# Hybrid attention and mLSTM layer on one Trainium2 core: the stages ahead of the MLP planned in 72 half-group slots

## What is computed

```python
xn = rmsnorm(x, ln1_w); z = xn @ w_in             # 28 column tiles of 128, and 8 gate columns
# z = [qa | ka | va | qm | km | vm | om | gates], four tiles each
# group A, 8 heads x 64: causal softmax attention over blocks of 256 (prompt: all of the past),
#   samples: top-3 blocks of the 1024 cached positions (8 pages of 128) and their own token
# group B, 4 heads x 128: mLSTM
qk = einsum('td,sd->ts', q, k) * W                # W = exp(D - m), causal
num = qk @ v + decay * (q @ C); den = qk.sum(-1) + decay * (q @ n)
h = num / maximum(abs(den), exp(-m)); C_new = dec_end * C + (w_end * k).T @ v
h = h * rsqrt(mean(h * h) + eps) * mlstm_norm_w * sigmoid(om)
x = x + concat(attn, h) @ w_out                   # 8 column tiles
x = x + square(relu(rmsnorm(x, ln2_w) @ w_up)) @ w_down   # 64 groups of 1024 x 128
y = rmsnorm(x, lnf_w)                             # also out: K, V, C, n, m of prompt and samples
```

## Time and profile before

| | |
|---|---|
| median, lowest and highest of 3 runs | 781.17, 781.05, 782.01 us |
| the profiled execution: its own time, its span | 782.44 us, 780.7 us |
| TensorE (PE) busy, granted clock | 96% of the span, 0.984 |
| VectorE (DVE), ScalarE (ACT), GpSimd (POOL) busy | 51%, 31%, 26% |
| read from and written to HBM | 92.92 MB, 6.64 MB |

### The profile page before, as it was taken

One profiled execution on the slowest core, in us unless ns is written; L12 is line 12 of the kernel. 1 busy time (PEld: TensorE's weight loads), 2 busy tenths in 40 slices (PEclk: granted clock), 3 DMA queues, 4 the chain that ended last, 5 costly groups with the idle time before them and its releaser, 6 DMA issues.

```text
span 780.7 us, 14774 instructions
## 1 busy us (share of the span) xinstructions
PE 750.3 (96%) x5781; PEld 696.1 (89%) x5781; DVE 397.2 (51%) x703; ACT 243.6 (31%) x407; POOL 204.3 (26%) x146
## 2 busy tenths in 40 slices
PE   6999998999999999889999999999989999999995
PEld 5999998979988755559999999999989999999994
DVE  3278987658876777432335433343333343343433
ACT  6242222133123444333524311333113321233213
POOL 4207996655332200013423200121002210022001
PEclk9999999789999999999999999999999999999998
DMA  6618876655421376663214233223322223313102
GB/s 219 214 58 255 264 240 218 206 147 184 132 96 61 103 207 215 193 225 113 89 34 147 66 100 108 87 76 108 109 76 90 77 87 108 109 56 108 55 1 110
DMA packets 84430, 100.54 MB, mean 129 GB/s; under 512 B 5262, under 2 KB 65250, under 8 KB 84362
## 3 DMA queue, kind: packets, MB, share of 16 engines
q1 hardware_dynamic: 73430, 92.91, 37.7%
q10 hardware_dynamic: 10932, 6.67, 2.8%
HBM read 92.92 MB, written 6.64 MB: 128 GB/s over the span
## 4 chain that ended last, share of the span: by engine, by line
PE 81%; DVE 5%; issue 4%; DMA 4%; SPq 3%; POOL 2%; ACT 1%; ACTq 0%; POOLq 0%; DVEq 0%
PE acc L593 23%; PE acc L594 23%; PE acc L595 23%; DMA kv<-in_cache_v_dram 2%; SPq L518 1%; PE acc L828 1%; SPq L524 1%; PE scr L894 1%; DMA raw<-in_w_in_dram 1%; PE scr L852 1%; POOL prod L1363 1%; PE scr L754 1%; PE scr L724 1%; PE scr L769 1%; PE scr L874 1%
## 5 line engine op out<-in xcount | busy, mean ns | idle before, releaser
L593 PE MATMUL acc<-act_hi,w_hi 128*128 128x260 f32 x960 | 275.7, 287 | 5.8 <-POOL w_lo L1007 3.0
L594 PE MATMUL acc<-act_lo,w_hi 128*128 128x260 f32 x960 | 273.3, 285 | 0.0
L595 PE MATMUL acc<-act_hi,w_lo 128*128 128x260 f32 x960 | 273.1, 284 | 0.0
L593 PEld LDWEIGHTS acc<-act_hi,w_hi 128*128 128x128 f32 x960 | 183.1, 191 | 8.3 <-issue 4.3
L1007 DVE TENSOR_TENSOR w_lo<-raw,w_hi 128x1024 fp32r<-128x1024 f32 x86 | 128.2, 1491 | 111.2 <-ACT w_hi L1000 109.7
L594 PEld LDWEIGHTS acc<-act_lo,w_hi 128*128 128x128 f32 x960 | 183.2, 191 | 0.4 <-issue 0.4
L595 PEld LDWEIGHTS acc<-act_hi,w_lo 128*128 128x128 f32 x960 | 183.1, 191 | 0.0
L1000 ACT ACTIVATE w_hi<-raw 128x1024 fp32r<-128x1024 f32 x100 | 105.2, 1054 | 182.8 <-PE acc L595 156.5
L593 PE MATMUL acc<-h_hi,w_hi 128*128 128x260 f32 x512 | 144.6, 282 | 0.0
L594 PE MATMUL acc<-h_lo,w_hi 128*128 128x260 f32 x512 | 144.5, 282 | 0.0
L595 PE MATMUL acc<-h_hi,w_lo 128*128 128x260 f32 x512 | 144.4, 282 | 0.0
(11 more groups left out here) (270 smaller groups left out, 820.0 us busy)
## 6 DMA issues: line engine op xcount, KB each, us to landing
kv<-in_cache_k_dram SPq DMA_DIRECT2D x64, 256.0 KB, 3.4
kv<-in_cache_v_dram SPq DMA_DIRECT2D x64, 256.0 KB, 3.0
raw<-in_w_up_dram SPq DMA_DIRECT2D x16, 1024.0 KB, 5.4
raw<-in_w_down_dram SPq DMA_DIRECT2D x16, 1024.0 KB, 5.1
raw<-in_w_in_dram SPq DMA_DIRECT2D x14, 1024.0 KB, 6.1
x_tok<-in_x_prompt_dram SPq DMA_DIRECT2D x8, 512.0 KB, 5.4
raw<-in_w_out_dram SPq DMA_DIRECT2D x4, 1024.0 KB, 5.1
Cs<-in_state_C_dram ACTq DMA_DIRECT2D x8, 256.0 KB, 5.8
```

Of the source, the lines that this page charges most:

```text
L593: pe.matmul(out, w_hi[:, slot, k, :], hi[k][:, cols], start=(n == 0), stop=False)
L594: pe.matmul(out, w_hi[:, slot, k, :], lo[k][:, cols], start=False, stop=False)
L595: mm = pe.matmul(out, w_lo[:, slot, k, :], hi[k][:, cols], start=False, stop=(n == KT - 1))
```

## The change

`plan()` makes one list for each of 72 **slots**. Slots 0 to 55 are the halves of the groups of `w_in`, slots 56 to 71 those of `w_out`, of which the first four are (28, half 0), (29, half 0), (28, half 1), (29, half 1). The order of `w_in` is now q, k, v of the attention, then q, k, v of each mLSTM head in turn, then the out-gates.

- Two heads of a tile `t` are attended together: `att_s` alternates between them, each on its 64 rows and with a bank of its own; one instruction adds the mask, takes the maximum and writes to SBUF; `att_p` normalises in SBUF; `att_t` are PE transposes; `att_o` alternates too, 64 wide each, into the two halves of one bank. Tiles start at slots 12, 20, 28 and 36.
- The mLSTM heads run from slots 27, 33, 39 and 45, 32 score chunks are in slots 10 to 31, `pv` in two halves of four pages in slots 38 to 55, the samples' mLSTM in 46 to 57. All 8 states have a place of their own; they are loaded in slots 31 and 45.
- `acc` is used as a ring of three banks; the fourth is for `pv`.
- VectorE makes the low parts up to group 19, GpSimd from group 20 (before: from 28).
- The out-gate is one `Sigmoid` on ScalarE and one multiply. High and low part of the mix are written where they are made.
- SP's loads are sorted by slot: weights, pages of keys and of values, two pages at a time.

```diff
-IN_ORDER = [c + t for c in (QA, QM, KM, VM, KA, VA, OM) for t in range(4)]
+COL = list(range(12)) + [c + h for h in range(MH) for c in (12, 16, 20)] + list(range(24, 28))
-DVE_LO = 28
+POOL_LO = 20
+HALVES = [(g, half) for g in range(N_IN) for half in range(2)]
+HALVES += [(G_OUT, 0), (G_OUT + 1, 0), (G_OUT, 1), (G_OUT + 1, 1)]
+HALVES += [(g, half) for g in range(G_OUT + 2, G_MLP) for half in range(2)]
+def chunk_slot(n):
+    return 10 + (2 * n + 1) // 3
+def pv_slot(b):
+    return 38 + 12 * b // 5
@@ plan
-    at(1, ("gates",))
-    at(2, ("rows",))
-    at(3, ("rows_m",))
-    at(4, ("qs_tok",), ("rows_end",))
-    at(5, ("qb", 0), ("qb", 1), ("gcols",))
+    at(2, ("gates", 0))
+    at(3, ("gates", 1))
+    at(4, ("rows",))
+    at(6, ("rows_m",))
+    at(8, ("qs_tok",), ("rows_end",))
+    at(9, ("qb", 0), ("qb", 1), ("gcols",))
+    for t in range(4):
+        at(11 + 2 * t, ("tokk", t))
+        at((18, 20, 23, 30)[t], ("tokv", t))
+        s = 12 + 8 * t
+        for n in range(3):
+            at(s + n, ("att_s", t, n))
+        for e in range(2):
+            at(s + 3 + e, ("att_p", t, e))
+            at(s + 5 + e, ("att_t", t, e))
...
+    at(33, ("gate",))
+    at(34, ("mx_t",), ("own",))
...
+    at(pv_slot(7) + 3, ("pv_end",))
...
+    at(57, ("sm_end",))
+    for n in range(4 * NS):
+        at(chunk_slot(n), ("score", *divmod(n, 4)))
+    for t in range(4):
+        at(20 + 8 * t, ("att_o", t), ("mix_att", t))
@@ PE
+            def half_gemm(i, parts, k_ready=None):
+                g, half = HALVES[i]
+                pe.wait_ge(s_w_lo_ok, g + 1)
+                if i >= 3:
+                    pe.wait_ge(s_acc_evac, i - 2)
+                for k in range(KT):
+                    if k_ready is not None:
+                        k_ready(k)
+                    three(acc[:, i % 3, 0:HALF], g % WSLOTS, parts, token_half(half), k, k)
@@ PE, qs_tok (unchanged; z_ready(g) is 2 * (g + 1))
                     pe.wait_ge(s_acc_evac, z_ready(QA + 3))
@@ PE, att_s
+                    outs = [open_job(pe, "att_s", t, n, e) for e in range(2)]
+                    for i, col in STEPS[n]:
+                        w = (i + 1) * P
+                        for e in range(2):
+                            lo = 64 * e
+                            mm = pe.matmul(outs[e][:, col:col + w], zT[lo:lo + 64, QA + t, i * P:(i + 1) * P],
                                            zT[lo:lo + 64, KA + t, 0:w], start=True, stop=True)
@@ PE, att_t and att_o
-                                mm = pe.matmul(out[:, col:col + P],
-                                               pr[:, h % 2, P_COL[i] + j * P:P_COL[i] + (j + 1) * P],
-                                               p_norm[:, h % 2, i, :], start=True, stop=True)
+                                mm = pe.transpose(out[:, col:col + P],
+                                                  pr[:, e, P_COL[i] + j * P:P_COL[i] + (j + 1) * P], ident[:, :])
-                        mm = pe.matmul(out[:, j * P:SEQ], v_tok[:, j, pair], pT[:, A_COL[j]:A_COL[j] + SEQ - j * P],
-                                       start=(j == 0), stop=(j == NT - 1))
+                        for e in range(2):
+                            mm = pe.matmul(out[64 * e:64 * e + 64, j * P:SEQ], v_tok[:, t % 2, j, 64 * e:64 * e + 64],
+                                           pTs[e][:, A_COL[j]:A_COL[j] + SEQ - j * P],
+                                           start=(j == 0), stop=(j == NT - 1))
@@ ScalarE, out-gate
-                    act.activation(o, o, ACT.Exp, scale=-1.0).then_inc(s_om_exp, 1)
+                    act.activation(zT[:, OM + h, :], zT[:, OM + h, :], ACT.Sigmoid).then_inc(s_om_sig, 1)
@@ VectorE, att_s and att_p
+                            ins = dve.tensor_tensor_reduce(
+                                out=pr[:, e, P_COL[i]:P_COL[i] + w], in0=out[:, col:col + w],
+                                in1=causal[:, SEQ - w:SEQ], scale=-ASCALE, scalar=-MASKED, op0=ALU.add, op1=ALU.min,
+                                accum_out=nmax[:, e, i:i + 1])
+                    for i in range(NT):
+                        p = pr[:, e, P_COL[i]:P_COL[i] + (i + 1) * P]
+                        ins = dve.tensor_scalar(p, p, rrec[:, e, i:i + 1], None, ALU.mult)
@@ VectorE, order of a slot
+            for s in range(N_HALVES):
+                n = s // 2 + AHEAD
+                if s % 2 == 0 and n < POOL_LO:
+                    weight_lo(dve, n, n % WSLOTS, n // 2 % 2)
+                if s < 2 * N_IN:
+                    evac_copy(s)
+                else:
+                    evac_out(s)
+                for name in TASKS[s]:
+                    task(*name)
@@ PE, ahead of slot 58
+                    if HALVES[i] == (G_OUT, 1):
+                        pe.wait_ge(s_smp_mix, 3)
```

More of the change, by code:

```diff
@@ new lines, with slot_of, z_ready, ml @@
+HALVES = [(g, half) for g in range(N_IN) for half in range(2)]
+HALVES += [(G_OUT, 0), (G_OUT + 1, 0), (G_OUT, 1), (G_OUT + 1, 1)]
+HALVES += [(g, half) for g in range(G_OUT + 2, G_MLP) for half in range(2)]
+N_HALVES = len(HALVES)
+LATE_X = 2
+def slot_of(g, half):
+    return HALVES.index((g, half))
+def z_ready(g):
+    return 2 * (g + 1)
+def ml(part, h):
+    return ML + 3 * h + part
+UNIT_PARTS = [1 if COL[2 * r + 1] == COL[2 * r] + 1 else 2 for r in range(N_IN // 2)] + [1] * (N_OUT // 2)
@@ L407, in build @@
         s_sm_pow = sem("sm_pow")
-        s_sm_end = sem("sm_end")
         s_ml_tri = sem("ml_tri")
@@ L493, in build @@
         Y_FIRST = {12: (0, 1), 13: (2, 3), 14: (NT,)}
+        HI = [QA + t for t in range(4)] + [ml(KM, h) for h in range(MH)]
+        LO = [KA + t for t in range(4)] + [ml(VM, h) for h in range(MH)]
         x_parts = tiles(act_hi), tiles(act_lo)
         h_parts = tiles(h_hi), tiles(h_lo)
-        mix_parts = tiles(mix_hi), tiles(mix_lo_att) + tiles(mix_lo_ml)
+        mix_parts = [mix[:, n, :] for n in HI], [mix[:, n, :] for n in LO]
         @block.sync
@@ L605, in main @@
                     bank_free(1)
-                    for n, k in enumerate(order):
-                        k_ready(n)
-                        three(0, n, k)
-                        three(1, n, k)
+                    for k in range(KT):
+                        k_ready(k)
+                        part(0, k)
+                        part(1, k)
                     return
@@ L612, in main @@
                     bank_free(half)
-                    for n, k in enumerate(order):
-                        if half == 0 and first_half is not None:
-                            first_half(n)
-                        three(half, n, k)
+                    for k in range(KT):
+                        part(half, k)
                     if half == 0 and between is not None:
@@ L1347, in task @@
             def task(name, *a):
-                if name == "weights":
-                    n = a[0] + AHEAD
-                    weight_lo(pool, n, n % WSLOTS, n // 2 % 2)
-                elif name == "rows":
-                    full(pool, "gates", 1)
-                    pool.memset(vm_tok[:, :, :, MD:MD + 1], 1.0).then_inc(s_vm_ones, 1)
-                elif name == "score":
+                if name == "score":
                     b, c = a
```

1107 lines of the change are left out of this document (559 added, 548 removed).

## The result

The changed kernel took 778.45 us (median of 10 runs, 775.87 to 780.5), the kernel before, on the same chips, 782.1 (10 runs, 780.57 to 783.84): ratio 0.9948, 95% interval 0.9929 to 0.9967. It is faster by 0.5%. The forecast was 760, and the range ended at 778. The profiled execution took 777.48 us; its span is 775.7.

A forecast was written before the change was run, and what follows sets the result against it. PE's own work was taken as the bound: 341 us ahead of the MLP plus 8, 12, 7 and 5 make 373, with 386.6 for the MLP 759.6 of span, median 760. Range 751 to 769; 8 in 10, 739 to 778.

The forecast's parts named there:

- (4): Earlier kernel's stage from 124 to 170 us, clock 0.81: its small matmuls are spread, 8.7 us come back.
- (a): Start: PE stands 6.3 us before `qs_tok`, waiting for slot 7's evacuation, plus 1.7 of low clock; 8 us added.
- (d): Slots 56 to 71: PE waits 4 us for `pv_end` and `sm_end`, 0.6 for evacuations before the MLP; 5 us added.
- (2): Two heads side by side on PE in `att_o` and `att_s`: 9.4 us saved in each.
- (3): Page loads spread over 18 slots: 15 us of PE's waits in the 260 to 346 us stage come back.
- the lock: Score stage: VectorE's `att_p` may wait for a whole GpSimd product through shared SBUF ports; 8 us taken, 47 at worst.
- (b): Score stage, slots 10 to 31: takes 104 us, 12 over PE's own work of 92, through VectorE and GpSimd.
- The slow rival: Score stage: GpSimd and VectorE block each other, all 20 `att_p` wait, stage takes 149 us; 805 us, chance 0.07.
- The rival named clock: Each `att_t` is followed by a half-clock spell, eight costing 2 us each; 776 us, chance 0.09.
- The smooth rival: VectorE keeps up; the score stage and slots 32 to 55 cost 3 us instead of 19; 744 us, chance 0.22.
- The rival without pairing: The two heads don't overlap on PE, so 7 to 12 us later; 769 us, chance 0.14.
- (c): Slots 32 to 55: `gate` on VectorE delays slot 34's evacuation and `mx_t`; 7 us added, bounds 0 and 20.

The follow-up runs named there:

- the kernel with all edits: Changed kernel with normalisation and copies of transposed probabilities on ScalarE, `ml_m` of head 0 ending slot 27, `pv_end` in slot 56, first `sm_r` ahead of `pv`; 761.22 us.
- e5_norm_start: Changed kernel with the normalisation on ScalarE, the gates' row work one slot later and score chunks not before slot 12; 771.94 us.
- e2_norm_act: Changed kernel with the normalisation of the probabilities moved from VectorE to ScalarE, VectorE keeping the reciprocal; 766.13 us.
- e1_start: Changed kernel with the gates' row work one slot later and score chunks not before slot 12; 780.05 us.
- e3_fill: Changed kernel with 40 unused matmuls put on PE in each of two gaps, in slots 8 and 57; 780.26 us.

## Why the prediction was wrong, point by point

**The account.** Forecast 341 us of PE work ahead of the MLP, 30.3 of waits, 1.7 of clock, and 386.6 behind: 759.6. The span is 775.7: 19.2 us more ahead of the MLP, 3.1 less behind. By the stage rows, with the waits taken as what PE isn't busy and the clock as (1 - granted) x length:

| | forecast | waits | clock | rest |
|---|---|---|---|---|
| slot 9 to 31, 114.5 us | 92 + 12 | 13.9 | 6.9 | 93.7 |
| slot 31 to the MLP, 214.1 us | 205.4, of which 12 waits | 10.6 | 10.7 | 192.8 |

(205.4 is 373 less 104 and the 63.6 at which slot 9 was emptied.) The waits are within 2 us of the forecast in each. The last two columns are not yet prices, since a low clock costs nothing while PE stands, and may cost a small matmul less than its share. The price is in traces where PE did the same work at a higher clock. From slot 9 to slot 31 the same 721 records kept PE busy 100.6 us at 0.94 and, with the products cut, 95.4 at 1.00. From slot 31 to the MLP the same 1504 records took 203.5 us at 0.95 (147.3 + 56.2 in the rows of the result) and 200.2 in the kernel with all edits:

```profile
166.60:375.20 208.60, 200.17 (x1504) 166.98 (x1504) 100.07 (x254) 69.81 (x128) 69.86 (x54) 0.99 0.53 160
```

So the clock cost PE some 5.3 + 3.3 = 8.6 us behind slot 9, not 17.6, and PE's work is 95.4 and about 200 us where the forecast had 92 and 193.4: 10 us more. With 0.5 us of waits that makes the 19.2.

**The first step that failed** is "(4) The low-clock stage: its small matmuls are spread, 8.7 us come back", with the clock's price in (a) to (d). The lost clock did not go, it grew from 8.5 to 20.5 us. I had the earlier trace rows and charged a spell only behind the start's gap, 1.7 us, where two windows lost 3.4; behind slot 9 the sum had nothing for some 9 us. The trace has six places where PE stands 2.6 us or more (2.0 and 1.3 in a row for one of them), and each has its spell, 1.6 to 3.4 us; the small matmuls of slots 50 to 53 have theirs too, 5.2 us from 292 to 316. Another trace has no spell behind a wait of 3.2 us (e5_norm_start and e2_norm_act above), so a wait makes a spell likely, not certain. What one costs is seen only on the spot: 2.8 us there, 2.7 and 2.4 where a gap was filled, nothing of it in the median.

**The second step that failed** is the 341 us of PE's work. Its 10 us too few are 1.6 at (2) and up to 4.7 at (3), see below; the rest isn't placed. Part of (4) may be in it, if the spread small matmuls gained less from the higher clock than the clock itself; no run tests that.

**Behind much of the waits and of the clock stands the lock.** With the products cut, waits and spells of the stage both go (98.0 us, clock 1.00), and the normalisation alone was worth 12.3 us. In (b) I sized the lock on `att_p` at 8 us, and four batches waited 7.5 (2.31, 2.08, 2.16 and 2.06 us for a first instruction of 0.28); low parts at 2.3, they took 2.28. So its length was right, and the working was wrong in another way: I added lengths on VectorE and took the stage as the longer of two sums and 4 us of slack. VectorE was busy only 97 of 114.5 us and PE 101: neither was full, since each waited for the other in turn. That the waits came out at 13.9 against 12 is luck in part. 6.4 of them are the one gap ahead of `ml_k` of head 0, which (b) didn't have; it stayed 6.4 us long with the normalisation on ScalarE and fell to 3.7 with `ml_m` behind the chunks. The slow rival's place and mechanism were the right ones; its price was wrong because only the first instruction of a batch waits, not all four.

**The rival named clock** gave 776, close to what came, but by another mechanism: a spell behind each `att_t`. With the products cut the stage holds four clusters of ten transposes and runs at 1.00, so transposes alone don't take the clock down. The Trainium skill's sentence in "TensorE: Matmul & The Clock Gate" (Part 4), that a transpose doesn't count as PE busy, is not refuted by this, but transposes aren't the cause of the low clock here. (The 275 ns that the prediction took from there are given for bf16; its 272 are of float32.) The smooth rival (744) is out for the changed kernel; with the lock removed and two queues mended the kernel came to 761.

**(1) and (2), the work removed.** Transposes 1.09 us for ten, as priced. `att_o` 2.30 for a pair (2.35 forecast), `att_s` 2.76: it saves 7.8 us of the 9.4, for which no row had stood. The rival without pairing is out.

**(3), the pages.** PE waits for pages 1.5 us in all, instead of 3.7, by the view of waits. That view misses most of it, because the records of matmuls that come late run into each other. The same 16 records of one sample's `pv` took 1.92 us when the pages were there and 3.83 when they weren't (timeline of the kernel before):

```profile
262.34 1.92 PE L828 MATMUL acc<-kv,S_wide 128*32 128x512 f32 x16
...
271.33 3.83 PE L828 MATMUL acc<-kv,S_wide 128*32 128x512 f32 x16
```

From the first record of a `pv` to the next other matmul, all eight took 27.9 us before and their sixteen halves 17.6 after. So 10.3 of the 15 us came back. Of the other 4.7, 2.9 are 24 matmuls of `w_out` in that stage, which the 71 us had left out; 1.8 I can't place.

**(a), the start.** The gap was 5.1 us (6.3 forecast), behind it 3.4 of clock: 8.5 against 8. Right in size; but that it adds to the rest was wrong. e1_start took it away and gained nothing in the median.

**(c) and (d).** Waits 10.6 against 12, at the places named: `gate` ahead of slot 34's evacuation (3.4) and `pv_end` with `sm_end` before slot 58 (5.6, not 4). There one instruction of 0.21 us took 2.30 beside GpSimd's low part (timeline of the kernel after, VectorE and GpSimd):

```profile
338.89 0.21 DVE L1818 TENSOR_TENSOR own_prod<-va_smp,own_p 64x32 f32<-64x32 f32 x1
...
340.00 2.30 DVE L1818 TENSOR_TENSOR own_prod<-va_smp,own_p 64x32 f32<-64x32 f32 x1
...
339.89 2.34 POOL L1083 TENSOR_TENSOR w_lo<-raw,w_hi 128x1024 fp32r<-128x1024 f32 x1
```

**The MLP** was 3.1 us shorter, which was no forecast of mine. In the profile of before PE waits 2.1 us once in it, at 582.23 us, with no releaser; of the other kernels' profiles only e3_fill's has such waits. I don't know what they are.

## What to carry to other kernels

Give a wait of TensorE a price for the half-clock spell that may follow it (here 2.4 to 2.8 us each on the spot), but don't expect it in the kernel's time before a run shows it: filling two gaps brought nothing, and taking away what caused the waits brought 17 us. Look whether TensorE's gaps are ended by an engine that is itself waiting. Where VectorE and GpSimd work in SBUF together, try the short VectorE instruction on ScalarE, even if VectorE isn't full: here it cost nearly a whole operation of GpSimd each time. Before you count a stage's waits from the view of waits alone, compare the same job with and without its data there. Two engines at 85 and 88% in a stage mean a chain of queues, not slack: find the instruction that stands at the head of a queue with others behind it, and move that one first.
